# A one-layer streaming encoder with a mixture of experts: an expert's slots in another order, and the last products on another engine

## The chip, the cores and the metric

The kernel runs on one core of one Trainium2 chip. Such a core has a matrix engine (TensorE, PE in the profile), three engines for elementwise work (VectorE = DVE, ScalarE = ACT, GpSimd = POOL), an engine that here only issues transfers (SyncE = SP), and 16 DMA engines that move data between HBM and the on-chip memory (SBUF). The metric is the device time of one execution in microseconds (us). Before the change it is 1167.24 us, the median of three runs (1166.24 to 1170.16).

## The reference

There are 1104 tokens of width 1024: 64 of a sample stream, 16 learned ones, and 1024 of a prompt. They pass through one layer. A token mixer comes first (an input projection, pooling windows, gated linear attention, an output projection), then a mixture of experts:

```python
p_group = softmax(x @ w_rg + b_rg)                    # 4 groups, the best one is taken
le_sel  = the 8 expert logits of that group           # (T, 8)
top_v, top_i = lax.top_k(softmax(le_sel), 2)          # two experts per token
gates   = p_g * top_v / sum(top_v)
h       = silu(xb @ w_eg[e]) * (xb @ w_eu[e])         # per expert e of 32: 1024 -> 512, twice
ys      = h @ w_ed[e]                                 # 512 -> 1024
out[token] = sum over its two experts of gate * ys
```

A last RMSNorm follows: `y * rsqrt(mean(y*y) + 1e-6) * norm_final`. All values are f32. Outputs are the normalized rows of prompt and sample and the new states of pooling and attention.

## The kernel before

The 1104 tokens and 48 padding rows stand in nine tiles of 128 rows (`TILES`; the first holds the sample, the padding and the 16 learned tokens). The program has three stages.

**Mixer and router** (to about 530 us): a loop over the tiles. For each tile DVE also works out, for both picks of each token, its expert and its rank, which is the number of earlier picks of that expert (`back_rank`, L915 to L930). A tile's normalized rows are stored to `hn_rows` in HBM, once for each pick. To turn ranks into lists, L929 compares each rank with the constant row `iota_block`, which has 96 entries (`BLOCK`), one for each slot of an expert. That gives a 0/1 matrix `at_rank` of tokens by slots, and the matrix engine multiplies it with a table of row numbers (`mark`, L1292 to L1296). Summed over the tiles this is `idx_i`, 96 slots by 32 experts: the row number of the pick in that slot, or `NO_ROW` (4096) where the slot is empty. The constant row holds 0, 1, ..., 95, so that rank r stands in slot r, and the empty slots are the last ones.

**Experts** (about 530 to 1115 us): one expert after the other, 0 to 31, with two sets of buffers, b = e mod 2.
- SP loads the three weight matrices, 2 MB each, into the arena (`load_weights`, L383 to L393): `w_eg` of expert e once the matrix engine is through with `w_eg` of expert e-2, and likewise `w_eu` and `w_ed`. So every weight transfer is issued when its buffer comes free, and the three of one expert stand in one queue behind each other.
- POOL issues two indirect transfers for each expert: `gather` (L470 to L475) reads the rows named by column e of `idx_i` from `hn_rows` into a buffer of 96 partitions, one slot to a partition; `scatter` (L477 to L486) writes the results of the 96 slots back to `pick_rows` in HBM. Both have `bounds_check` with `oob_is_err=False`: a slot with `NO_ROW` moves no row.
- The matrix engine transposes the rows (L1149), multiplies by `w_eg` and `w_eu` (`up`, L1369) and by `w_ed` (`down`, L1380 and L1386). ACT and DVE form silu and the products in between, ACT takes the result out of PSUM.

There is code for experts with more than 96 picks (`slots`, `table`, the blocks under `n_x > 0`). With the given inputs the router gives every expert 50 to 88 picks, 2208 in all, so these blocks are jumped over.

**Last stage** (from about 1115 us): SP loads the two result rows of each token (L429), 18 transfers. For every tile DVE adds them, weighted with the gates, to the residual (`combine`, two instructions, L1125 and L1127). ACT squares and sums the row and forms 1/rms (L722 to L724). For tiles 0, 2, 4, 6 and 8 DVE multiplies by 1/rms and by `norm_final` in one instruction (`normalize`, L1133). For tiles 1, 3, 5 and 7 ACT multiplies by 1/rms (L727) and POOL by `norm_final` (L523). SP stores the tiles in order (L433, L435), each when its semaphore `out_ready` is up.

Of the kernel before, what the change touches and what calls it, by code (L numbers as in the profile page):

```python
# [24 lines left out]
ALU = mybir.AluOpType  # L25
ACT = mybir.ActivationFunctionType
# [10 lines left out]
TILES = (SAMPLE + PADS + META + SEQ) // P  # L37
# [21 lines left out]
BLOCK = 96  # L59
# [5 lines left out]
PICK_ROWS = PICKS * TILES * P  # L65
OUT_ROWS = [SAMPLE] + [P] * (TILES - 1)
NO_ROW = 4096
BIG = 3.0e38

# [19 lines left out]
def constants():  # L90
    c = np.zeros((P, N_CONST), np.float32)
    p = np.arange(P)[:, None]
    t = np.arange(P)[None, :]

    def put(name, v):
        c[:, COL[name][0]:COL[name][1]] = v

    put("ident", p == t)
    put("keep", np.arange(PAIRS * P)[None, :] % CHUNK != 0)
    put("causal", (p <= t) & (p // CHUNK == t // CHUNK))  # L100
    put("before", p < t)
    put("count_fix", np.concatenate([w / np.minimum(np.arange(META) + 1, w) for w in WINDOWS])[None, :])
    put("iota_block", np.arange(BLOCK)[None, :])
    put("iota_e", np.arange(NE)[None, :])
    put("first_g", GROUPS - np.arange(GROUPS)[None, :])
    put("first_e", PER_GROUP - np.arange(PER_GROUP)[None, :])
    put("pick", p + TILES * P * np.arange(PICKS)[None, :] - NO_ROW)
    put("valid", (p < SAMPLE) | (p >= SAMPLE + PADS))
    put("block_edge", BLOCK * (1 + np.arange(EXTRA_PER_E))[None, :])
    put("iota_x", np.arange(EXTRA)[None, :])  # L110
    put("edge_x", BLOCK * np.arange(EXTRA)[None, :])
    return c
# [40 lines left out]
def build(nc, x_all, state_pool, state_gla, norm_mix, w_in, w_gate_up, b_gate, w_pool, pool_scale, gla_norm, w_out,  # L153
# [5 lines left out]
    with ExitStack() as ctx:  # L159
        def sb(name, shape, dt=F32):  # L160
            return ctx.enter_context(nc.sbuf_tensor(name, shape, dt))

        def sem(name):
            return ctx.enter_context(nc.semaphore(name))
# [15 lines left out]
        def con(name, rows=P):  # L180
            return cst[0:rows, COL[name][0]:COL[name][1]]
# [114 lines left out]
        def lot(n):  # L296
            return arena[:, n * D:(n + 1) * D]
        y1 = [lot(2 * i) for i in range(TILES)]
        y2 = [lot(2 * i + 1) for i in range(TILES)]
        g_fin = lot(2 * TILES)  # L300
        fss = sb("fss", [P, TILES])
# [10 lines left out]
            parted dve_front dve_back dve_once dve_moe dve_fin act_front act_back act_once act_fin history_kept pool_steps  # L312
            pe_eT pe_g pe_u2 pe_d sig_ready hid_ready eT_ready ye_ready row_idx_ready
            x_tab_dve x_tab_pe x_idx_ready x_w x_rows x_pe x_dve x_act x_stored x_pool pick_idx_ready
            fin_ready frstd_ready scaled_ready g_fin_in""").split()
        s = {n: sem(n) for n in names}
        g_in = [sem(f"g_in{b}") for b in range(2)]
        u_in = [sem(f"u_in{b}") for b in range(2)]
# [4 lines left out]
        out_ready = [sem(f"out_ready{i}") for i in range(TILES)]  # L323
# [116 lines left out]
        def _(pool):  # L440
# [77 lines left out]
                                                     bounds_check=PICK_ROWS - 1, oob_is_err=False).then_inc(s["x_stored"], 16)  # L518
                        wait_parted(pool, s["x_stored"], 16 * n + 16, s["parted"])

            for i in range(1, TILES, 2):
                pool.wait_ge(s["scaled_ready"], (i + 1) // 2)
                nc.gpsimd.tensor_tensor(y2[i], y2[i], g_fin, ALU.mult).then_inc(out_ready[i], 1)  # L523

        @block.scalar
        def _(act):
            A = nc.scalar.activation
# [3 lines left out]
            final = Steps(act, s["act_fin"])  # L532
# [186 lines left out]
            for i in range(TILES):  # L719
                act.wait_ge(s["fin_ready"], i + 1)  # L720
                r = OUT_ROWS[i]
                final.then(A(y2[i][0:r, :], y1[i][0:r, :], ACT.Square, scale=D ** -0.5, accum_out=fss[0:r, i:i + 1]))  # L722
                final.then(A(fss[0:r, i:i + 1], fss[0:r, i:i + 1], ACT.Ln, bias=eps[0:r, 0:1]))
                rstd_i = A(fss[0:r, i:i + 1], fss[0:r, i:i + 1], ACT.Exp, scale=-0.5)  # L724
                if i % 2:
                    final.then(rstd_i)
                    A(y2[i], y1[i], ACT.Copy, scale=fss[:, i:i + 1]).then_inc(s["scaled_ready"], 1)  # L727
                else:
                    rstd_i.then_inc(s["frstd_ready"], 1)

        @block.vector
        def _(dve):
# [13 lines left out]
            V.tensor_copy(token[:, :], con("pick")).then_inc(s["setup_dve"], 1)  # L747
            V.memset(idx_f[:, :], float(NO_ROW)).then_inc(s["idx_added"], 1)
            def x_turned(i, first=False):

                if not first:
                    dve.wait_ge(s["pe_v"], i)
                for half in range(2):
                    dve.wait_ge(s["pe_xT"], 2 * i + half + 1)
                    k = slice(half * KD // 2, (half + 1) * KD // 2)
                    V.tensor_tensor(xnT[:, k, :], bank[half][:, :].rearrange("p (k n) -> p k n", n=P),
                                    g_mix[:, k].unsqueeze(2).to_broadcast([P, KD // 2, P]), ALU.mult).then_inc(s["xnT_ready"], 1)
# [115 lines left out]
            def first_of(step, values, top, order, marks, out, valid=None):  # L873

                step.then(V.tensor_reduce(top, values, AX.X, ALU.max))
                step.then(V.scalar_tensor_tensor(out=marks, in0=values, scalar=top, in1=order, op0=ALU.is_ge, op1=ALU.mult))
                step.then(V.tensor_reduce(rt[:, 0:1], marks, AX.X, ALU.max))
                if valid is None:
                    step.then(V.tensor_scalar(out, marks, rt[:, 0:1], None, ALU.is_equal))
                else:  # L880
                    step.then(V.tensor_scalar(out, marks, rt[:, 0:1], valid, ALU.is_equal, ALU.mult))

            def back_route(j, first=False):
# [9 lines left out]
                first_of(back, le[:, 0, :], rt[:, 2:3], con("first_e"), le[:, 2, :], oh[:, 0, :])  # L893
                back.then(V.scalar_tensor_tensor(out=le[:, 1, :], in0=oh[:, 0, :], scalar=-BIG, in1=le[:, 0, :], op0=ALU.mult, op1=ALU.add))
                first_of(back, le[:, 1, :], rt[:, 3:4], con("first_e"), le[:, 3, :], oh[:, 1, :])
# [170 lines left out]
            once.then(V.tensor_copy(token[:, :], con("pick")))  # L1066
            once.then(V.memset(idx_xf[:, :], float(NO_ROW)))

# [51 lines left out]
            final = Steps(dve, s["dve_fin"])  # L1120
# [7 lines left out]
                                       op0=ALU.mult, op1=ALU.add).then_inc(s["fin_ready"], 1)  # L1128

            def normalize(i):  # L1130
                dve.wait_ge(s["frstd_ready"], i // 2 + 1)
                r = OUT_ROWS[i]
                V.scalar_tensor_tensor(out=y2[i][0:r, :], in0=y1[i][0:r, :], scalar=fss[0:r, i:i + 1], in1=g_fin[0:r, :],  # L1133
                                       op0=ALU.mult, op1=ALU.mult).then_inc(out_ready[i], 1)

            dve.wait_ge(s["g_fin_in"], 16)
            for i in range(TILES):
                combine(i)
                if i % 2:
                    normalize(i - 1)  # L1140
            normalize(TILES - 1)

# [349 lines left out]
```

## Time and profile before

| what | value |
|---|---|
| median of three runs | 1167.24 us |
| the profiled execution: its time, its span | 1166.75 us, 1164.9 us |
| PE busy | 1042.9 us, 90% of the span |
| DVE, ACT, POOL busy | 426.3, 247.0, 118.8 us |
| moved by DMA | 262.08 MB, mean 225 GB/s |
| weights of one expert | 3 x 2048 KB |

The span runs from the first to the last instruction, and the execution's own time is 1.85 us longer. The profile gives busy time by engine, 40 equal slices of the span (29.1 us each) with the share in which the 16 DMA engines were busy, and the chain of work that ended last, followed back from the end. "DMA share" in a table of stretches is the mean busy share of the 16 DMA engines; packets that overlap on one engine can bring it a little over 1.

### The profile page before, as it was taken

The numbers are of one execution on the slowest core, as the hardware profiler recorded it, in microseconds if no ns is written. First come the engines' busy times: TensorE is split into PE (matmuls) and PEld (weight loads), VectorE is DVE, ScalarE is ACT, GpSimd is POOL, SyncE is SP. The second block draws the span as 40 slices with busy tenths as digits, with TensorE's granted clock in tenths as the row PEclk, the third lists the DMA queues.
The fourth block names the chain that finished last, engine by engine and source line by source line (L and its number), as shares of the span: only waits on it lengthen the run. The fifth ranks groups of instructions, "written<-read, shape, count | busy, mean of one in ns | idle before, by whom it ended". The sixth has DMA issues, their size and how long they took to land.

```text
span 1164.9 us, 31332 instructions
## 1 busy us (share of the span) xinstructions
PE 1042.9 (90%) x13842; PEld 853.9 (73%) x13842; DVE 426.3 (37%) x914; ACT 247.0 (21%) x510; POOL 118.8 (10%) x178
## 2 busy tenths in 40 slices
PE   5999999999999999866999999998988888899910
PEld 5778786868687777636888988897877777787810
DVE  1426162625345362622523322332313132322347
ACT  2333232222323131210111111111111101010124
POOL 0110101010010101001111111111110101010012
PEclk9999999999999999977999999999999999999965
DMA  8900000000000000574999999999999999999566
GB/s 280 360 1 37 0 36 36 0 36 0 36 0 36 0 36 1 205 306 157 376 379 390 391 400 380 387 390 368 370 370 356 374 353 372 353 372 353 214 240 246
DMA packets 50844, 262.08 MB, mean 225 GB/s; under 512 B 8205, under 2 KB 10701, under 8 KB 42618
## 3 DMA queue, kind: packets, MB, share of 16 engines
q1 hardware_dynamic: 41050, 234.05, 53.2%
q0 software_dynamic: 7168, 18.10, 4.6%
q10 hardware_dynamic: 2592, 9.44, 2.0%
q8 instruction: 26, 0.43, 0.1%
q14 instruction: 8, 0.07, 0.0%
HBM read 241.84 MB, written 26.80 MB: 231 GB/s over the span
## 4 chain that ended last, share of the span: by engine, by line
PE 62%; DMA 24%; DVE 10%; issue 2%; ACT 1%; SPq 0%; ACTq 0%; DVEq 0%; POOLq 0%; POOL 0%
DMA arena<-in_w_eg 22%; PE bank L1369 19%; PE bank L1161 17%; PE bank L1270 11%; PE bank L1380 5%; PE bank L1386 2%; PE bank L1149 2%; DVE er L815 2%; PE bank L1239 2%; DVE arena L1125 1%; DVE arena L1127 1%; DMA arena<-in_w_in 1%; PE bank L1263 1%; DVE hnT L870 1%; PE bank L1257 1%
## 5 line engine op out<-in xcount | busy, mean ns | idle before, releaser
L1161 PEld LDWEIGHTS bank<-xnT,arena 128*128 128x128 f32 x1728 | 198.0, 193 | 11.8 <-issue 7.6
L1161 PE MATMUL bank<-xnT,arena 128*128 128x128 f32 x1728 | 199.3, 277 | 3.7 <-DMA arena<-in_w_in 3.7
L1369 PEld LDWEIGHTS bank<-xnT,arena 128*64 128x64 f32 x4096 | 171.1, 138 | 16.0 <-DMA arena<-in_w_eg 9.9
L1369 PE MATMUL bank<-xnT,arena 128*64 128x96 f32 x4096 | 174.2, 248 | 8.8 <-DMA arena<-in_w_eg 7.1
L1369 PEld LDWEIGHTS bank<-hnT,arena 128*64 128x64 f32 x4096 | 169.9, 137 | 14.2 <-issue 14.2
L1369 PE MATMUL bank<-hnT,arena 128*64 128x96 f32 x4096 | 172.8, 246 | 7.0 <-DMA arena<-in_w_eg 6.9
L1009 DVE TENSOR_SCALAR mixT<-mixT 128x384 f32<-128x384 f32 x32 | 11.5, 361 | 355.0 <-ACT mixT L685 355.0
L1270 PE MATMUL bank<-arena,mixT 128*128 128x512 f32 x288 | 126.9, 599 | 2.9 <-DVE mixT L856 2.9
L1270 PEld LDWEIGHTS bank<-arena,mixT 128*128 128x128 f32 x288 | 54.7, 192 | 69.3 <-issue 65.6
L1380 PE MATMUL bank<-arena,osq 128*32 128x384 f32 x768 | 88.2, 495 | 9.0 <-DMA arena<-in_w_ed 9.0
L1380 PE MATMUL bank<-arena,silu_r 128*32 128x384 f32 x768 | 85.8, 488 | 7.6 <-DMA arena<-in_w_ed 7.1
L1386 PE MATMUL bank<-arena,osq 128*32 128x256 f32 x384 | 87.7, 385 | 0.0
L1386 PE MATMUL bank<-arena,silu_r 128*32 128x256 f32 x384 | 85.9, 380 | 0.0
L1010 DVE RECIPROCAL mixT<-mixT 128x384 f32<-128x384 f32 x32 | 81.7, 2553 | 1.1
L1211 PE MATMUL bank<-arena,xnT 128*128 128x512 f32 x144 | 65.3, 597 | 0.0
L861 DVE TENSOR_TENSOR h_all<-bank,h_all 128x512 f32 (+1 forms) x9 | 6.2, 692 | 145.6 <-PE bank L1270 145.6
L690 ACT ACTIVATE kz_v<-bank 96x384 f32<-96x384 f32 x32 | 13.8, 482 | 187.2 <-PE bank L1386 187.2
L453 POOL TENSOR_TENSOR window_work<-window_work 128x568 f32<-128x568 f32 x9 | 10.2, 1132 | 422.5 <-ACT window_work L583 422.5
L1386 PEld LDWEIGHTS bank<-arena,osq 128*32 128x32 f32 x384 | 41.4, 111 | 15.5 <-issue 0.8
L690 ACT ACTIVATE hs<-bank 96x384 f32<-96x384 f32 x32 | 13.8, 482 | 181.3 <-PE bank L1386 181.3
L1386 PEld LDWEIGHTS bank<-arena,silu_r 128*32 128x32 f32 x384 | 41.0, 110 | 15.0
L1380 PEld LDWEIGHTS bank<-arena,osq 128*32 128x32 f32 x768 | 31.7, 111 | 20.3 <-issue 11.3
(197 smaller groups left out, 1030.0 us busy)
## 6 DMA issues: line engine op xcount, KB each, us to landing
arena<-in_w_eg SPq DMA_DIRECT2D x32, 2048.0 KB, 28.3
arena<-in_w_eu SPq DMA_DIRECT2D x32, 2048.0 KB, 28.1
arena<-in_w_ed SPq DMA_DIRECT2D x32, 2048.0 KB, 27.9
hn_rows<-hs ACTq DMA_DIRECT2D x18, 512.0 KB, 3.4
arena<-pick_rows SPq DMA_DIRECT2D x16, 512.0 KB, 10.3
arena<-in_w_in SPq DMA_DIRECT2D x3, 2048.0 KB, 14.6
arena<-in_w_out SPq DMA_DIRECT2D x1, 4096.0 KB, 25.0
out_y_prompt<-arena SPq DMA_DIRECT2D x8, 512.0 KB, 2.8
```

Of the source, the lines that this page charges most:

```text
L690: A(ye[b][:, half * OWN:(half + 1) * OWN], bank[6 + half][0:BLOCK, 0:OWN], ACT.Copy).then_inc(s["ye_ready"], 1)
L815: front.then(V.reciprocal(flat, flat))
L870: V.tensor_tensor(hnT[:, k, :], bank[half][:, :].rearrange("p (k n) -> p k n", n=P), g_ffn[:, k].unsqueeze(2).to_broadcast([P, KD // 2, P] ...
L1010: moe.then(V.reciprocal(gs[:, 0:NH], gs[:, 0:NH]))
L1149: return nc.tensor.transpose(out, src, ident[0:n, 0:n])
L1161: last = mm(out, w_in_sb[:, k, a:b], xnT[:, k, :], start=k == 0, stop=k == KD - 1)
L1211: last = mm(bank[6][:, :], xnT[:, k, :], w_in_sb[:, k, V0:R0], start=k == 0, stop=k == KD - 1)
L1239: last = mm(out[:, 2 * p * DV:(2 * p + 2) * DV], kz[:, c, p, :], v_sb[:, 2 * p * DV:(2 * p + 2) * DV], start=True, stop=True)
L1270: last = mm(bank[half][:, :], mixT[:, k, :], w_out_sb[:, k, half * 512:(half + 1) * 512], start=k == 0, stop=k == KD - 1)
L1369: last = mm(out[q * SW:(q + 1) * SW, n * BLOCK:(n + 1) * BLOCK], w[:, k, m * P + q * SW:m * P + (q + 1) * SW], rowsT[b][:, k, :], start=k ...
L1380: last = mm(bank[6 + half][g * TG:(g + 1) * TG, 0:OWN], tokens(k, g), wd[b][:, k, half * OWN:(half + 1) * OWN], start=k == 0, stop=k == KF ...
L1386: return mm(bank[n][TGS * TG:P, c:c + REST], tokens(k, g), wd[b][:, k, 2 * OWN:D], start=k == 0 and c == 0, stop=k == KF - 1, skip_group_c ...
```

## The change

Two things are changed. The constant row `iota_block` now holds 16 * (s mod 6) + s div 6 for slot s. Rank r therefore stands in slot 6 * (r mod 16) + r div 16: rank 0 in slot 0, rank 1 in slot 6, rank 15 in slot 90, rank 16 in slot 1. Before, 69 picks filled slots 0 to 68; now they fill the first five of the six slots 6n to 6n+5 for n = 0 to 4, and the first four for n = 5 to 15. The instructions that make and use the lists stay the same. In the last stage POOL's four products and ACT's four scalings go, and DVE normalizes all nine tiles.

```diff
+SPREAD = 16
+RUN = BLOCK // SPREAD
...
-    put("iota_block", np.arange(BLOCK)[None, :])
+    put("iota_block", (SPREAD * (np.arange(BLOCK) % RUN) + np.arange(BLOCK) // RUN)[None, :])
...
-            for i in range(1, TILES, 2):
-                pool.wait_ge(s["scaled_ready"], (i + 1) // 2)
-                nc.gpsimd.tensor_tensor(y2[i], y2[i], g_fin, ALU.mult).then_inc(out_ready[i], 1)
...
-                rstd_i = A(fss[0:r, i:i + 1], fss[0:r, i:i + 1], ACT.Exp, scale=-0.5)
-                if i % 2:
-                    final.then(rstd_i)
-                    A(y2[i], y1[i], ACT.Copy, scale=fss[:, i:i + 1]).then_inc(s["scaled_ready"], 1)
-                else:
-                    rstd_i.then_inc(s["frstd_ready"], 1)
+                A(fss[0:r, i:i + 1], fss[0:r, i:i + 1], ACT.Exp, scale=-0.5).then_inc(s["frstd_ready"], 1)
...
             def normalize(i):
-                dve.wait_ge(s["frstd_ready"], i // 2 + 1)
+                dve.wait_ge(s["frstd_ready"], i + 1)
...
             for i in range(TILES):
                 combine(i)
-                if i % 2:
+                if i:
                     normalize(i - 1)
             normalize(TILES - 1)
```

On DVE in the last stage, the end of the program before, from the second instruction of tile 6 on (L1125 and L1127 combine, L1133 normalizes; `arena` holds the rows, `gate_all` the gates, `fss` 1/rms):

```order
L1127 SCALAR_TENSOR_TENSOR arena<-arena,gate_all 128x1024
L1125 SCALAR_TENSOR_TENSOR arena<-arena,gate_all,h_all 128x1024
L1127 SCALAR_TENSOR_TENSOR arena<-arena,gate_all 128x1024
L1133 SCALAR_TENSOR_TENSOR arena<-arena,fss 128x1024
L1125 SCALAR_TENSOR_TENSOR arena<-arena,gate_all,h_all 128x1024
L1127 SCALAR_TENSOR_TENSOR arena<-arena,gate_all 128x1024
L1133 SCALAR_TENSOR_TENSOR arena<-arena,fss 128x1024
```

The same place now, where the lines are L1119, L1121 and L1127:

```order
L1121 SCALAR_TENSOR_TENSOR arena<-arena,gate_all 128x1024
L1127 SCALAR_TENSOR_TENSOR arena<-arena,fss 128x1024
L1119 SCALAR_TENSOR_TENSOR arena<-arena,gate_all,h_all 128x1024
L1121 SCALAR_TENSOR_TENSOR arena<-arena,gate_all 128x1024
L1127 SCALAR_TENSOR_TENSOR arena<-arena,fss 128x1024
L1119 SCALAR_TENSOR_TENSOR arena<-arena,gate_all,h_all 128x1024
L1121 SCALAR_TENSOR_TENSOR arena<-arena,gate_all 128x1024
L1127 SCALAR_TENSOR_TENSOR arena<-arena,fss 128x1024 x2
```

A normalizing instruction now stands behind every pair from tile 1 on, and at the end stand those of tiles 7 and 8; there are four more of them in all. On ACT the end of the program before, tiles 7 and 8 (L722 squares and sums, L723 and L724 form 1/rms, L727 scales the row):

```order
L722 ACTIVATE arena,fss<-arena 128x1024
L723 ACTIVATE fss<-fss,eps 128x1
L724 ACTIVATE fss<-fss 128x1
L727 ACTIVATE arena<-arena,fss 128x1024
L722 ACTIVATE arena,fss<-arena 128x1024
L723 ACTIVATE fss<-fss,eps 128x1
L724 ACTIVATE fss<-fss 128x1
```

The same two tiles now:

```order
L721 ACTIVATE arena,fss<-arena 128x1024
L722 ACTIVATE fss<-fss,eps 128x1
L723 ACTIVATE fss<-fss 128x1
L721 ACTIVATE arena,fss<-arena 128x1024
L722 ACTIVATE fss<-fss,eps 128x1
L723 ACTIVATE fss<-fss 128x1
```

The scaling between the tiles is gone, and POOL's last instructions, `L523 TENSOR_TENSOR arena<-arena 128x1024 x4`, with it. The order on PE and SP is the same as before.

## Rows read from the trace of the kernel before

**Rows 1.** The page: its slices' DMA lines, and the chain that ended last.
```profile
DMA  8900000000000000574999999999999999999566
GB/s 280 360 1 37 0 36 36 0 36 0 36 0 36 0 36 1 205 306 157 376 379 390 391 400 380 387 390 368 370 370 356 374 353 372 353 372 353 214 240 246
...
PE 62%; DMA 24%; DVE 10%; issue 2%; ACT 1%; SPq 0%; ACTq 0%; DVEq 0%; POOLq 0%; POOL 0%
```

**Rows 2.** The chain in order of time: start us, us, what.
```profile
606.34 10.71 PE bank L1369 x256
623.18 10.71 PE bank L1369 x256
640.02 10.71 PE bank L1369 x256
...
673.69 10.71 PE bank L1369 x256
...
774.73 5.46 PE bank L1369 x128
780.34 31.24 DMA arena<-in_w_eg
811.63 5.53 PE bank L1369 x128
817.32 31.93 DMA arena<-in_w_eg
...
1094.81 10.71 PE bank L1369 x256
```

**Rows 3.** Stretches: us, busy us of each engine (instructions), PE clock, DMA share, GB/s.
```profile
570.00:780.00 210.00, 209.47 (x4180) 182.71 (x4174) 66.61 (x96) 31.83 (x77) 31.34 (x51) 1.00 1.01 387
780.00:1060.00 280.00, 250.50 (x4915) 217.17 (x4912) 78.14 (x105) 35.30 (x85) 33.82 (x58) 0.99 0.99 366
```

**Rows 4.** Issues of w_eg at 595, 763 and 840-860 us: KB, us to landing.
```profile
arena<-in_w_eg SPq DMA_DIRECT2D x1, 2048.0 KB, 12.8
...
arena<-in_w_eg SPq DMA_DIRECT2D x1, 2048.0 KB, 29.2
...
arena<-in_w_eg SPq DMA_DIRECT2D x1, 2048.0 KB, 32.2
```

**Rows 5.** SP in order of time: one issue of w_eg.
```profile
645.63 0.33 SPq L385 DMA_DIRECT2D arena<-in_w_eg  x1
```

**Rows 6.** The page's DMA queues: packets, MB, time as share of 16 engines' span.
```profile
q1 hardware_dynamic: 41050, 234.05, 53.2%
q0 software_dynamic: 7168, 18.10, 4.6%
```

**Rows 7.** Stretches of 2 us with and without row transfers, columns as in rows 3.
```profile
630.00:632.00 2.00, 2.00 (x56) 2.00 (x52) 2.00 (x1) 0.00 (x0) 0.00 (x0) 1.00 1.02 412
...
634.00:636.00 2.00, 2.00 (x30) 1.50 (x33) 1.32 (x3) 0.00 (x0) 0.00 (x0) 1.00 1.01 299
...
640.00:642.00 2.00, 2.00 (x51) 2.00 (x52) 0.00 (x0) 1.86 (x5) 0.00 (x0) 1.00 1.00 412
...
915.00:917.00 2.00, 2.00 (x54) 2.00 (x52) 1.52 (x3) 0.00 (x0) 0.00 (x0) 1.00 1.00 334
...
921.00:923.00 2.00, 2.00 (x32) 1.42 (x28) 0.00 (x0) 0.00 (x0) 0.00 (x0) 1.00 0.97 305
```

**Rows 8.** POOL's gather issued at 628.31 us: us to landing.
```profile
xs<-hn_rows,rows_idx POOLq DMA_INDIRECT x1, 9.5
```

**Rows 9.** Last stage in order of time: start us, us, engine, line, operation, idle before.
```profile
1123.39 1.28 DVE L1125 SCALAR_TENSOR_TENSOR arena<-arena,gate_all,h_all 64x1024 f32<-64x1024 f32 x1 [15.86 <-DMA arena<-pick_rows]
...
1129.60 1.27 DVE L1125 SCALAR_TENSOR_TENSOR arena<-arena,gate_all,h_all 128x1024 f32<-128x1024 f32 x1
...
1131.50 2.90 POOL L523 TENSOR_TENSOR arena<-arena 128x1024 f32<-128x1024 f32 x1 [16.20 <-ACT arena L727]
1132.11 3.38 DVE L1125 SCALAR_TENSOR_TENSOR arena<-arena,gate_all,h_all 128x1024 f32<-128x1024 f32 x1
...
1155.88 1.28 DVE L1127 SCALAR_TENSOR_TENSOR arena<-arena,gate_all 128x1024 f32<-128x1024 f32 x1
1156.45 2.91 POOL L523 TENSOR_TENSOR arena<-arena 128x1024 f32<-128x1024 f32 x1 [5.41 <-ACT arena L727]
...
1158.94 1.51 DVE L1133 SCALAR_TENSOR_TENSOR arena<-arena,fss 128x1024 f32<-128x1024 f32 x1 [1.78 <-ACT fss L724]
```

**Rows 10.** Last stage by line: xcount, busy us, mean ns, idle before.
```profile
L1125 DVE SCALAR_TENSOR_TENSOR arena<-arena,gate_all,h_all 128x1024 f32<-128x1024 f32 (+1 forms) x9 | 17.8, 1975 | 15.9 <-DMA arena<-pick_rows 15.9
```

**Rows 11.** SP's loads of the result rows, and the stretch that they fill.
```profile
1117.83 11.23 SPq L429 DMA_DIRECT2D arena<-pick_rows  x18
...
1120.00:1140.00 20.00, 0.00 (x0) 0.00 (x0) 16.44 (x12) 8.88 (x18) 3.09 (x2) 0.50 1.01 386
```

More of the change, by code:

```diff
@@ L314, in build @@
             x_tab_dve x_tab_pe x_idx_ready x_w x_rows x_pe x_dve x_act x_stored x_pool pick_idx_ready
-            fin_ready frstd_ready scaled_ready g_fin_in""").split()
+            fin_ready frstd_ready g_fin_in""").split()
         s = {n: sem(n) for n in names}
```

## The prediction

> **What bounds the kernel now.** I read the page first: the slices, then the chain of waits. The DMA engines are 90% busy or more from slice 20 to slice 37, and the chain puts 62% of the span on PE and 24% on DMA [rows 1]. A mean over stages with different limits says little, so the chain in order of time came next [rows 2]. It changes its nature in the middle of the expert stage. Up to 774.73 us every expert starts 16.84 us after the one before (606.34 to 774.73 us is ten experts): PE is bound by its own work. After that, every second expert ends on a 31 to 33 us wait for `w_eg`, and the starts of experts 14 and 31, at 774.73 and 1094.81 us, lie 17 experts and 320.1 us apart, 18.83 us each. At PE's own pace they would lie 286.3 us apart. So 33.8 us is the most that faster transfers can give in this stage.
>
> Why does DMA fall behind only then? The time from issue to landing of `w_eg` answers it [rows 4]. An issue waits for its buffer, so in PE's rhythm it comes a fixed time before its use: that of 645.63 us is for the expert that starts at 673.69 us, 28.1 us later [rows 5, 2]. It lands after 12.8 us for expert 5 and after 29.2 us for expert 15. So each expert's weights land 1.64 us later than the last, and DMA's pace is 16.84 + 1.64 = 18.48 us per expert from the start; the lead is merely used up at expert 15. In the stretches the DMA share stays at 1.01 and 0.99, while the rate falls from 387 to 366 GB/s [rows 3]. Work, or disturbance, on the engines that finish last is therefore what can be won.
>
> The last stage is a third regime: from 1123.39 us DVE runs without a gap, apart from one wait of 1.78 us before its last instruction [rows 9].
>
> **The order of the slots.** Nothing is added in this stage: the constant has other values, and the same instructions read it. What can move is which DMA engine carries which row. The POOL queue shows 7168 packets and 18.10 MB [rows 6]. 7168 is 64 transfers of 112; 18.10 MB is 4416 rows of 4 KB, and the router's counts, worked out from the given inputs, sum to 2208 picks, moved twice. So an empty slot moves no row, but has a packet, and 112 is 96 slots and one more packet for each of 16 engines. 
>
> The Trainium skill ("DMA: Bandwidth & Descriptors", "Why a DMA increments its semaphore by 16 and not by 1") gives consecutive shares: a DMA of 96 partitions uses 16 engines, the first share on the lowest-numbered; no run here shows it. Another section of the page, "The descriptor swizzle", has a formula for 128 partitions that would give the first eight engines eight slots each and the others four; by it the busiest engine would go from 16 rows to about 11.5, and the result would be that of the first rival.
>
> A row's price: 4.6% of 16 engines' 1164.9 us is 857 us for 4416 rows, 0.194 us each [rows 6]. 2.5 rows fewer are 0.485 us per expert. All of it lies on the engines that end last, if the mapping holds.
>
> The rows also disturb. In stretches of 2 us in which none is on its way the rate is 412 GB/s; towards the end of a gather that was issued at 628.31 us and landed 9.5 us later it is 299, and in the late half stretches at 305 and 334 GB/s lie further apart [rows 7, 8]. How much is that? The busiest engine moves 6.29 MB / 16 + 12 x 4 KB = 442 KB per expert; at a sixteenth of 412 GB/s that is 17.18 us, and 18.48 is what it takes: 1.30 us of disturbance. With at most 4.75 rows instead of 6 in a transfer I let it shrink in that ratio, by 0.27 us. The bounds are nothing, and all of 1.30, since engines in step might not disturb each other; growth is the last rival. I take the value near the lower end, because the number of rows stays the same.
>
> New pace: 18.48 - 0.485 - 0.27 = 17.72 us, 0.88 more than PE's. From expert 5 to 31 the landing time grows 26 x 0.88 = 22.9 us to 35.7 us, 7.6 more than the 28.1 that PE can bear. Expert 31 starts 33.8 - 7.6 = **26.2 us earlier**. With nothing off the disturbance it is 19.0 us, with most of it gone all 33.8. The wait that replaces the present one is the same, for `w_eg`, from about expert 22 on.
>
> **The last stage.** Three of POOL's four products each stall a DVE instruction: the one at 1132.11 us takes 3.38 instead of 1.28 us and ends 1.1 us behind POOL's product, which had started 0.6 us earlier [rows 9]. By line, L1125 has 17.8 us where nine of 1.28 are 11.5: 6.3 us of stalls [rows 10]. The fourth product costs the last normalization 0.23 us (1.51 against 1.28). On the other side stand four more normalizations of DVE. Five of its instructions, from 1123.39 to 1129.60 us, take 6.21 us, 1.242 each. Before the last tile's pair ends there are now 18 + 7 of them: 31.05 us, to 1154.44 us, where it is 1157.16 now. The last normalization still waits 1.78 us behind the pair for ACT, with that of tile 7 hidden in the wait; it starts at 1156.22 and ends at 1157.50 instead of 1160.45 us: **2.9 us earlier**. The other new waits, for 1/rms of the odd tiles, cost nothing: it is there 1.78 us after a pair, and another pair (2.48 us) stands in between; only the next pair is queued behind. POOL's and ACT's removed work is off the path otherwise. The loads are no new bound: 18, 8.9 MB, at 386 GB/s end near 1141 us, and the last tile's pair starts at 1152 [rows 11]. If tile 7's normalization were not covered, 1.2 us would be lost. The bounds are 0.5 us (stores now one by one on DVE's rhythm) and 4 us.
>
> **Sum.** Against the profiled execution's own 1166.75 us (span 1164.9 and 1.85 around it): 1166.75 - 26.2 - 2.9 = 1137.6 us. The median of the runs is 0.5 us higher, so **1138 us**.
>
> **Rivals.**
> 1. PE's pace throughout. With the engines in step most of the disturbance goes, and the pace is under 16.84 us. For it: 412 GB/s would bring an expert's 6.86 MB in 16.65 us. Against it: the disturbed stretches are there at 634 us already [rows 7], before the lead is used up. 1166.75 - 33.8 - 2.9 + 0.5 = 1130.5 us. Chance 0.22.
> 2. Nothing is won in the expert stage: DMA is bound by bytes, or the slots are already dealt out evenly. For it: a DMA share of 0.99 leaves little that could be filled, and the bytes are the same. Against it: 387 GB/s over 210 us at the same share shows that 366 is no ceiling [rows 3]. Only the last stage gains: 1164.3 us. Chance 0.10. The Trainium skill ("HBM Reference", "Specifications (TRN2)") puts the effective rate per core at about 358 GB/s, by which this rival would hold; the 387 measured goes beyond that, and the page itself says that a core streaming alone does.
> 3. Slower: the rows now come on all 16 engines, so that no engine's weights run undisturbed. If the stretch near 325 GB/s grows from some 8 us of an expert's time (915 to 923 us) to 16, each expert loses 8 x (1 - 325/412) = 1.7 us against 0.49 gained; the pace from the start becomes 19.7 us, and expert 31 is 26 x 2.86 + 12.8 - 28.1 = 59 us late instead of 33.8: about 1189 us. It decides from a stretch 2.3 us longer than now. Against it: fewer rows per engine make a transfer shorter. Chance 0.05.
> 4. Part of it: the row time alone or less, 1145 to 1160 us. Chance 0.18.
>
> My forecast's own case, 1132 to 1145 us, has 0.45. The range that leaves out 2 in 10 is 1129 to 1157 us. About 0.3% (3.5 us) is what a measurement of this kernel tells from no change; rival 2 lies inside it, so: faster 0.85, within 0.10, slower 0.05.
>
> **What would show it.** In the changed profile the landing time of `w_eg` for expert 15 should be 20 to 23 us instead of 29.2, the stretch from 570 to 780 us stay near 390 GB/s, and that from 780 to 1060 us come close to it; the first long wait for `w_eg` should stand behind expert 20. If the landing time grows as before, the mapping or the mechanism is wrong. If it does not grow, rival 1 holds. If the rate is lower in both stretches, rival 3 does. In the last stage all 18 L1119 and L1121 should take 1.28 us, and DVE's last instruction 1.28.

## The result, and the profile after

The changed kernel takes 1128.56 us (median of four runs, 1128.18 to 1130.37), the kernel before 1166.74 us (median of four runs, 1164.63 to 1170.16). The ratio is 0.967, with an interval from 0.965 to 0.970. The forecast was 1138 us with a range from 1129 to 1157 us: the direction was right, the gain, 38 us, was a third larger than the 28.7 that were forecast, and the time lies just below the low end. PE's pace throughout, the outcome of the first rival, is what happened, though not in the way that the rival gave for it (below).

The profiled execution after took 1130.37 us, with a span of 1128.4 us. The page's slices and chain come first, as those of [rows 1].

```profile
DMA  8900000000000000076799999999999999999557
GB/s 277 384 2 38 0 37 0 37 0 37 16 21 37 0 37 1 38 299 218 254 397 367 406 404 402 413 408 396 409 402 398 411 405 396 412 397 395 238 198 304
...
PE 84%; DVE 10%; DMA 2%; issue 2%; ACT 1%; SPq 0%; ACTq 0%; DVEq 0%; POOLq 0%; POOL 0%
```

The DMA engines look as busy as before, and yet DMA has gone from 24% of the chain to 2%. The rate no longer falls in the second half of the expert stage; it stays near 400 GB/s. The chain in order of time (start us, us, what) shows the same at the first multiplication of an expert:

```profile
608.37 10.71 PE bank L1363 x256
625.21 10.71 PE bank L1363 x256
...
776.76 10.71 PE bank L1363 x256
793.60 10.71 PE bank L1363 x256
...
1063.02 10.71 PE bank L1363 x256
```

Experts 4 and 31 start at 608.37 and 1063.02 us. That is 27 experts in 454.65 us, 16.84 us each: PE's own pace up to the last expert. The waits for `w_eg` of 31 to 33 us in [rows 2] are gone. PE's list of waits between 530 and 1080 us (line, releaser: us in total, times, longest us) names no weights at all; its one DMA wait is for the first expert's rows:

```profile
PE bank L1143 <- DMA window_work<-hn_rows,rows_idx: 5.9, 1, 5.9
PE bank L1363 <- issue: 2.0, 3, 1.2
PE bank L1374 <- issue: 1.0, 2, 0.5
```

In the kernel before, the same list, between 540 and 1112 us, began with the weights:

```profile
PE bank L1380 <- DMA arena<-in_w_ed: 16.1, 14, 2.0
PE bank L1369 <- DMA arena<-in_w_eg: 14.0, 15, 1.2
```

The two stretches of [rows 3] now read (columns as there):

```profile
570.00:780.00 210.00, 209.28 (x4156) 181.83 (x4147) 68.25 (x99) 31.87 (x77) 29.19 (x49) 1.00 1.01 398
780.00:1060.00 280.00, 280.00 (x5601) 245.25 (x5601) 88.49 (x119) 40.31 (x97) 39.57 (x66) 1.00 1.01 401
```

The DMA share is 1.01 in both, where it was 1.01 and 0.99, while the rate rose from 387 to 398 and from 366 to 401 GB/s.

In the last stage every one of DVE's combining and normalizing instructions now takes 1.28 us, and the last normalization waits 0.58 us where it waited 1.78 [rows 9, 10]. By line (xcount, busy us, mean ns, idle before):

```profile
L1121 DVE SCALAR_TENSOR_TENSOR arena<-arena,gate_all 128x1024 f32<-128x1024 f32 (+1 forms) x9 | 11.6, 1284 | 0.3
L1127 DVE SCALAR_TENSOR_TENSOR arena<-arena,fss 128x1024 f32<-128x1024 f32 (+1 forms) x9 | 11.5, 1279 | 0.6 <-ACT fss L723 0.6
L1119 DVE SCALAR_TENSOR_TENSOR arena<-arena,gate_all,h_all 128x1024 f32<-128x1024 f32 (+1 forms) x9 | 11.5, 1277 | 15.5 <-DMA arena<-pick_rows 15.5
```

The first combining instruction and the last two normalizations, in order of time:

```profile
1091.22 1.28 DVE L1119 SCALAR_TENSOR_TENSOR arena<-arena,gate_all,h_all 64x1024 f32<-64x1024 f32 x1 [15.46 <-DMA arena<-pick_rows]
...
1122.22 1.28 DVE L1127 SCALAR_TENSOR_TENSOR arena<-arena,fss 128x1024 f32<-128x1024 f32 x1
...
1124.09 1.28 DVE L1127 SCALAR_TENSOR_TENSOR arena<-arena,fss 128x1024 f32<-128x1024 f32 x1 [0.58 <-ACT fss L723]
```

So the 36.5 us between the two spans (1164.9 and 1128.4) come out as follows. The first combining instruction starts 32.2 us earlier (1123.39 and 1091.22). From there to the end of the last normalization it is 37.06 us before and 34.15 after: 2.9 us. From there to the end of the span it is 4.45 us before and 3.03 after: 1.4 us more.

### The profile page after: what moved, and what is told of

It is laid out like the page before. It is cut to its first block, busy times and chain, and to the rows that moved or that the text cites. A ratio compares the mean times of both kernels' runs of the same rounds, so it can differ in the third digit from the quotient of the medians.

```text
span 1128.4 us, 31328 instructions
## 1 busy us (share of the span) xinstructions
PE 1041.3 (92%) x13842; PEld 853.4 (76%) x13842; DVE 424.4 (38%) x918; ACT 242.5 (21%) x506; POOL 107.2 (10%) x174
## 4 chain that ended last, share of the span: by engine, by line
PE 84%; DVE 10%; DMA 2%; issue 2%; ACT 1%; SPq 0%; ACTq 0%; DVEq 0%; POOLq 0%; POOL 0%
PE bank L1363 31%; PE bank L1155 17%; PE bank L1264 11%; PE bank L1374 10%; PE bank L1380 5%; PE bank L1143 4%; DVE er L809 2%; PE bank L1233 2%; DVE arena L1121 1%; DVE arena L1119 1%; DVE arena L1127 1%; DMA arena<-in_w_in 1%; PE bank L1257 1%; DVE hnT L864 1%; PE bank L1251 1%
## 5 line engine op out<-in xcount | busy, mean ns | idle before, releaser
L1380 PEld LDWEIGHTS bank<-arena,osq 128*32 128x32 f32 x384 | 40.8, 110 | 15.0
L1205 PEld LDWEIGHTS bank<-arena,xnT 128*128 128x128 f32 x144 | 26.1, 190 | 26.3 <-issue 26.3
```

The lines of the kernel that those rows point to most:

```text
L1205: last = mm(bank[6][:, :], xnT[:, k, :], w_in_sb[:, k, V0:R0], start=k == 0, stop=k == KD - 1)
L1380: return mm(bank[n][TGS * TG:P, c:c + REST], tokens(k, g), wd[b][:, k, 2 * OWN:D], start=k == 0 and c == 0, stop=k == KF - 1, skip_group_c ...
```

## The experiments

Unless said otherwise, an edit stands against the changed kernel. Ratios are against the kernel before, run beside it on the same chip; its medians there were 1162 to 1165 us.

### One part of the change at a time

`slots_only` is the kernel before with the new `iota_block`; `tail_only` is the changed kernel with the old one:

```diff
-    put("iota_block", (SPREAD * (np.arange(BLOCK) % RUN) + np.arange(BLOCK) // RUN)[None, :])
+    put("iota_block", np.arange(BLOCK)[None, :])
```

> The kernel before with the new order of the slots alone; the last stage stays as it was. Theory A (the DMA engine with the most rows sets when weights land; the new order brings it from 12 rows per expert to 9.5, and DMA then keeps PE's pace): about 33 us less than before, 1133 to 1136 us, with no wait of PE for w_eg, and the landing time of w_eg no longer growing. Theory B (the two parts need each other): less than 30 us.

> The changed kernel with the old order of the slots (rank r in slot r), so the last stage's part alone. From the two traces: DVE's work from first combine to last normalization 37.06 -> 34.15 us, and from its end to the end of the span 4.45 -> 3.03 us. So 3 to 4.5 us less than before, 1162 to 1164 us. If the shorter end after DVE's last instruction belongs to the expert stage and not to the last stage, 3 us or less.

`slots_only` took 1132.07 us, ratio 0.973 (0.971 to 0.975), and PE waited for no weights. `tail_only` took 1159.36 us, ratio 0.995 (0.994 to 0.997). So the order of the slots brings 31 to 33 us (1159.36 to 1128.56; 1164.74 to 1132.07), and the last stage 3.5 to 5.4 us (1132.07 to 1128.56; 1164.74 to 1159.36): the expert stage's gain is the slots' alone.

`slots_only` also has the landing times that the trace after lacks for `w_eg`. Its DMA issues in windows about 578, 746 and 982 us (experts 5, 15 and 29; KB, us to landing) read, one row each:

```profile
arena<-in_w_eg SPq DMA_DIRECT2D x1, 2048.0 KB, 13.4
...
arena<-in_w_eg SPq DMA_DIRECT2D x1, 2048.0 KB, 14.8
...
arena<-in_w_eg SPq DMA_DIRECT2D x1, 2048.0 KB, 18.0
```

Where [rows 4] grow from 12.8 to 29.2 us in ten experts, this grows by 4.6 us in 24, 0.19 us per expert. DMA's pace is then 16.84 + 0.19 = 17.03 us per expert, where 17.72 had been forecast. It is still slower than PE, but of the 28.1 us of lead the stage leaves about ten unused. (The lead is the time from the issue of `w_eg` to its use in PE's rhythm.)

### How many engines carry six rows

These three keep every instruction and every row, and deal the slots out in other ways (the names behind `#` are not part of the code). `reverse` mirrors the old order, so that the last engines are full and the first one empty. `spread8` lets used and skipped slots alternate too, but in twelves: with 69 picks eight or nine slots are used, then four or three skipped, so that, in blocks of six, eight of the 16 engines have six rows. `one_heavy` gives the first six ranks to the first six slots and deals the rest out evenly: one engine has six rows, the others four or five.

```diff
+    put("iota_block", (BLOCK - 1 - np.arange(BLOCK))[None, :])                                # reverse
+    put("iota_block", (8 * (np.arange(BLOCK) % 12) + np.arange(BLOCK) // 12)[None, :])        # spread8
+    slot = np.arange(BLOCK)                                                                  # one_heavy
+    put("iota_block", np.where(slot < RUN, slot, RUN + (SPREAD - 1) * (slot % RUN) + slot // RUN - 1)[None, :])
```

> The changed kernel with rank r in slot 95 - r: the used slots stand together at the end instead of the beginning, so the rows are as uneven over blocks of six slots as in the kernel before (six rows in the busiest block, none in the emptiest), but they lie in other partitions. Theory A (the busiest of 16 engines, each serving six neighbouring slots): as the last stage's part alone, 1160 to 1166 us. Theory C (which SBUF partitions the gathered rows are written to sets the disturbance: slots 0 to 68 are half of the partitions again and again): a large part of the gain, 1130 to 1150 us.

> The changed kernel with consecutive ranks twelve slots apart instead of six (rank r in slot 12 * (r mod 8) + r div 8): used and empty slots alternate and lie over all 96 partitions, but of each pair of blocks of six the first is always full and the second has about 2.6 rows. Theory A (the busiest engine's row count): 12 rows per expert as before, so hardly better than the last stage's part alone, 1155 to 1166 us. Theory D (it is the mixing of used and empty slots, or their spread over all partitions, that helps): as the changed kernel, 1127 to 1133 us. If engines serve twelve slots or slots one by one, it would be near the changed kernel too.

> The changed kernel, but the first six slots are always full (ranks 0 to 5) and the other ranks are dealt over the other fifteen blocks of six: engine 0 has 12 rows per expert as in the old order, every other engine about 8.4. Theory A (the row count of the busiest engine alone): as the last stage's part alone, about 1159 us. Theory E (the price is the disturbance while many engines are out of step and many rows meet, and one engine more or less does little): near the changed kernel, 1128 to 1140 us. Both in part: between, with the landing of the weights late by what one engine's 2.5 rows cost, 0.5 us per expert.

`reverse` took 1146.93 us (0.984, from 0.981 to 0.987), `spread8` 1151.12 us (0.990, from 0.988 to 0.992), `one_heavy` 1129.21 us (0.970, from 0.967 to 0.973). `reverse` lies in the range of the theory that partitions matter, which a run below tests; `spread8` lies 4 us below the range of the theory of the busiest engine. Alternation of used and skipped slots is not what counts in the main: `spread8` alternates and gets back 8 of the 31 us. Its issues of `w_ed` at 587.22 and 755.61 us, ten experts apart, land after

```profile
arena<-in_w_ed SPq DMA_DIRECT2D x1, 2048.0 KB, 15.3
...
arena<-in_w_ed SPq DMA_DIRECT2D x1, 2048.0 KB, 25.4
```

that is 1.01 us later per expert, a pace of 17.85 us. In the kernel before, the two of 589.68 and 758.08 us were

```profile
arena<-in_w_ed SPq DMA_DIRECT2D x1, 2048.0 KB, 12.8
...
arena<-in_w_ed SPq DMA_DIRECT2D x1, 2048.0 KB, 27.9
```

or 18.35, and after, those of 591.73 and 995.86 us, 24 experts apart,

```profile
arena<-in_w_ed SPq DMA_DIRECT2D x1, 2048.0 KB, 12.4
...
arena<-in_w_ed SPq DMA_DIRECT2D x1, 2048.0 KB, 16.8
```

or 17.02.

For `one_heavy`, whose time alone would say that a full engine costs nothing, the view has the landing of every second `w_ed` only. Its issues of 608.02, 776.42 and 1012.17 us (experts 5, 15 and 29) land after

```profile
arena<-in_w_ed SPq DMA_DIRECT2D x1, 2048.0 KB, 13.7
...
arena<-in_w_ed SPq DMA_DIRECT2D x1, 2048.0 KB, 17.1
...
arena<-in_w_ed SPq DMA_DIRECT2D x1, 2048.0 KB, 31.1
```

that is 0.34 us later per expert at first, 1.00 in the fourteen experts after, and 0.73 over all 24, a pace of 17.57. After the change, the same three experts' issues (608.56, 776.95 and 1012.70 us) land after

```profile
arena<-in_w_ed SPq DMA_DIRECT2D x1, 2048.0 KB, 13.8
...
arena<-in_w_ed SPq DMA_DIRECT2D x1, 2048.0 KB, 13.7
...
arena<-in_w_ed SPq DMA_DIRECT2D x1, 2048.0 KB, 17.5
```

or -0.01 us per expert at first and 0.15 over all 24. And the PE of `one_heavy`, by the list of waits up to 1090 us, does begin to wait for weights, but only in experts 28 and 29, 2.8 us in all:

```profile
PE bank L1375 <- DMA arena<-in_w_ed: 1.9, 2, 1.0
...
PE bank L1364 <- DMA arena<-in_w_eg: 0.9, 2, 0.5
```

So a single engine with six rows costs 0.35 us per expert over the first ten of these experts and 0.73 - 0.15 = 0.58 over all 24; the price forecast for 2.5 rows on the busiest engine (0.485) lies between the two. The lead of the transfers covers nearly all of it: 24 times 0.58 us is 14 us, about ten were left over, and the waits are the rest. My theory in its plain form, that the time follows the busiest engine, failed on this run; the pace follows it, the time only where the lead is gone. With a mean of 69 picks, none, one, eight and eleven engines with six rows (the changed kernel, `one_heavy`, `spread8`, the kernel before) go with 16.83, 17.18, 17.85 and 18.35 us over ten experts (4 to 14 or 5 to 15).

`reverse` remains odd. Its counts per engine are those of `tail_only`, eleven with six rows, its rates 390 and 379 GB/s against 387 and 369, and it is 12 us faster; its time lies near that of `spread8` with eight. So the number of full engines is not all. Which of them are full matters somewhat; these runs do not say why.

### The price of the rows with DMA as the bound

To read DMA's own pace, PE must not set the rhythm. In the kernels named `half_` the gate and up products of an expert take half of their steps:

```diff
-                    for k in range(KD):
+                    for k in range(KD // 2):
```

Each is a single execution. The pace is the time between SP's issues of `w_eg` for experts 15 and 31, divided by 16. In `half_old` and `half_new`, for example (start us, us, queue):

```profile
751.72 3.90 SPq L388 DMA_DIRECT2D arena<-in_w_eg  x1
...
1048.34 4.05 SPq L388 DMA_DIRECT2D arena<-in_w_eg  x1
```

```profile
746.91 0.95 SPq L388 DMA_DIRECT2D arena<-in_w_eg  x1
...
1027.77 0.65 SPq L388 DMA_DIRECT2D arena<-in_w_eg  x1
```

which are 18.54 and 17.55 us per expert. `half_none` has no rows at all (`iota_block` is -1), `half_old_gather` and `half_old_scatter` have the old order and rows in one of the two transfers alone, with a list of empty slots for the other.

> The old order of the slots, and TensorE leaves out half of the products with w_eg and w_eu (four of eight parts of the inner dimension), so that PE needs some 11.5 us per expert and DMA is bound all through the expert stage; all transfers stay. It shows DMA's own pace. Starts of experts 5 and 31 should be 18.5 to 18.9 us per expert apart, as in the late half of the kernel before.

> The same with the new order: DMA's own pace, which the changed kernel hides behind PE's 16.84 us. The prediction's sum says 17.7 us per expert, which the changed kernel already contradicts. Theory A with the rows' price alone: 18.0. Theory E (most of the disturbance goes with engines in step): 16.2 to 16.8 us, and rates over 400 GB/s.

> The same with all slots empty: the constant row holds -1, so no rank matches, gathers and scatters are issued but move no row, and the last stage loads the rows of the normalized input instead. It shows the weights' own pace, the floor under both orders. At 412 GB/s (stretches without rows of the kernel before) 6.29 MB take 15.3 us per expert. If the old order's pace over this floor is near 12 rows of 0.19 us (2.3 us), the rows cost what their packets take and do not disturb; if it is 3.3 us or more, a third of their price is disturbance.

> As half_old (half of the products with w_eg and w_eu left out, DMA bound all through; 18.54 us per expert between the issues of w_eg for experts 15 and 31, with no rows 15.01), but the scatters move no row (their list of slots is all empty) and the last stage loads the rows of the normalized input. If the gather makes the whole disturbance: 15.0 + 6 rows of 0.16 to 0.19 us + 1.3 to 1.5 = about 17.4 us. If gather and scatter share alike: 16.8 us.

> As half_old, but the gathers move no row (their list is all empty, the matrix engine works on what lies in the buffers). If the gather makes the whole disturbance: 15.0 + 6 rows = 16.0 to 16.2 us per expert. If they share alike: 16.8 us. If it is the scatter: 17.4 us.

| kernel | us per expert | whole kernel, us |
|---|---|---|
| `half_none` | 15.01 | 1053.0 |
| `half_old_scatter` | 15.79 | 1075.3 |
| `half_new_gather` | 16.76 | 1101.7 |
| `half_full_gather` | 17.45 | 1124.7 |
| `half_old_gather` | 17.46 | 1117.7 |
| `half_new` | 17.55 | 1123.7 |
| `half_heavy` | 17.81 | 1132.5 |
| `half_reverse` | 18.08 | 1137.6 |
| `half_old_shift32` | 18.09 | 1150.7 |
| `half_old` | 18.54 | 1151.5 |

Of the expectations, `half_new` misses Theory E's range and comes nearest to the prediction's own 17.7, and `half_old_gather` fits a gather that makes the whole disturbance. The weights alone take 15.01 us. Old scatters add 0.78 us, old gathers 2.45 us. The rate in stretches of 2.5 us from 800 to 900 us, first of `half_old_scatter`, then of `half_old_gather`, shows what kind of cost it is:

```profile
GB/s 423 406 400 419 444 424 433 419 388 415 442 441 421 416 377 395 436 441 418 429 415 398 413 462 411 426 431 344 408 456 428 433 416 387 411 444 438 418 429 406
```

```profile
GB/s 315 369 428 431 369 405 444 418 403 298 339 356 398 406 298 329 393 426 393 413 447 346 311 315 390 406 402 411 290 339 395 408 336 388 447 439 343 298 346 362
```

With scatters the rate runs more evenly: one stretch of the 40 lies under 370 GB/s, with gathers eighteen do. From 740 to 960 us (columns as in [rows 3]) `half_none` and then `half_old_scatter` have the same 419 GB/s, so that scatters add little but their bytes:

```profile
740.00:960.00 220.00, 174.07 (x3048) 139.38 (x3048) 72.26 (x100) 37.13 (x90) 32.80 (x57) 1.00 1.01 419
```

```profile
740.00:960.00 220.00, 174.13 (x2898) 137.65 (x2894) 71.85 (x98) 34.81 (x84) 32.63 (x56) 0.95 1.01 419
```
With gathers the rate breaks down to about 300 GB/s about once per expert. The disturbance of [rows 7] is in the main the gather's; gather and scatter alone add 3.23 us together, and both at once 3.53.

The new order brings the price of the gather from 2.45 to 1.75 us (`half_new_gather`), 0.71 of it, near the 4.75 / 6 = 0.79 of the rows on the busiest engine. Is it that engine's count, or the number of rows, or that some engines have none? `half_full_gather` is `half_old_gather` with an entry in all 96 slots, so that nearly every engine moves six rows; two entries point past the end, and 94 rows are moved for each expert (12.33 MB on the POOL queue in 32 transfers):

```diff
-    put("pick", p + TILES * P * np.arange(PICKS)[None, :] - NO_ROW)
+    put("pick", p + TILES * P * np.arange(PICKS)[None, :])
...
-            V.memset(idx_f[:, :], float(NO_ROW)).then_inc(s["idx_added"], 1)
+            V.tensor_copy(idx_f[:, :], con("pick", BLOCK)[:, 0:1].to_broadcast([BLOCK, NE])).then_inc(s["idx_added"], 1)
```

> As half_old_gather (17.46 us per expert; 2.45 over the 15.01 without rows), with the new order. If a gather's price goes by the rows of the busiest engine (4.75 instead of 6): 15.01 + 2.45 x 0.79 = 16.95. If it goes by the number of rows in all (the same 69): 17.46. If engines with equal work stay in step and disturb each other for a shorter time: less than 16.8.

> As half_old_gather, but the empty slots are filled: their entries name a row of their own, and all entries are moved on by their slot's number (so other rows are gathered; a few past the end are left out). Every engine then gathers six rows for each expert, 96 in all instead of 69, and none is idle. By the rows of the busiest engine: 17.46 as half_old_gather. By the number of rows in all: 15.01 + 2.45 x 96 / 69 = 18.4. If being in step is worth more than the added rows cost: under 17.3.

`half_full_gather` has 17.45 us, with 94 rows, as `half_old_gather` has 17.46 with 69; both issue `w_eg` of expert 31 within 2 us of each other (1024.76 and 1022.90 us). The whole kernels differ by 7 us, 5 of them behind that issue and not explained. In these two runs the count of the fullest engines sets the gather's price; rows added on the others cost next to nothing.

The prediction took its mapping, six neighbouring slots to an engine, without a view. The Trainium skill ("DMA: Bandwidth & Descriptors", "Why a DMA increments its semaphore by 16 and not by 1") gives a DMA of 96 partitions 16 engines, the first share on the lowest-numbered, and does not say how the slots of an indirect transfer are shared out. The paces above agree with six neighbouring slots, but they do not refute the other mapping that the prediction names: by it the gathers of `half_full_gather` and `half_old_gather` also have equally many rows, eight, on their fullest engines, and one, three and eight engines have eight in `one_heavy`, `spread8` and the old order. The trace decides between them. In the first gather of `half_full_gather`, from 530.36 to 532.22 us, no other queue moves anything, and its record holds 94 packets of 4 KB and 18 of 4 bytes. Linked where one packet starts within 5 ns of another's end, they form runs, one engine's packets in a row. At least five of these, more by how near ties are linked, are exactly six rows with one 4-byte packet behind, and none has the eight rows that the other mapping asks for.

Another rival was that not engines but the places in memory that the rows land in matter. `half_old_shift32` moves the gathered rows from partitions 0 to 95 to partitions 32 to 127:

```diff
-                nc.gpsimd.indirect_dma_start(rows[b], None, hn_dram, ...
+                nc.gpsimd.indirect_dma_start(rows[b][P - BLOCK:P, :], None, hn_dram, ...
```

> As half_old, but the gathered rows are written to partitions 32 to 127 instead of 0 to 95 (the matrix engine turns them with a product that picks these partitions): every DMA engine has the same rows as in half_old, only the place in SBUF differs; with about 69 of 96 slots used it is partitions 32 to 100 instead of 0 to 68. Theory C (which partitions are written sets the disturbance): 17.3 to 18.0 us per expert instead of 18.54. Theory A or F: 18.4 to 18.7 us.

It issued the weights of expert 31 at 1048.57 us, `half_old` at 1048.34, and the whole kernels differ by 0.8 us. By this run the partitions make no difference. The two paces, 18.09 and 18.54, differ through the first of the two marks (759.09 and 751.72 us): issues come in uneven pairs, so a pace from one execution is sure to some 0.4 us. By the issues of `w_ed` for the same experts the two are 18.36 and 18.52.

> As half_new (17.55 us per expert), with the order of one_heavy: engine 0 has 12 rows per expert, the others about 8.4. If the busiest engine's packets are what counts there: 17.55 + 2.5 x 0.19 = 18.0. If nothing: 17.55. If one straggler is enough to bring all of the old order's price back: 18.5.

> As half_old (18.54 us per expert), with the order of reverse (slot 95 - r): as many rows on the busiest engines, other partitions and other engines. If row counts are all: 18.5. The run reverse was 12 us faster than tail_only, so if that belongs to DMA's own pace: about 18.0.

`half_heavy` (`one_heavy`'s order) lies 0.26 us above `half_new`, less than expected and within that uncertainty; by the issues of `w_ed` it is 0.67 (17.99 and 17.32). `half_reverse` lies 0.46 us below `half_old`, 0.60 by `w_ed` (17.92 and 18.52); its whole time, 14 us shorter, supports `reverse`, without a cause.

### Shorter packets of weights

If a row of 4 KB loses because it takes turns with larger packets, smaller ones should help the old order. `old_4k` is `tail_only` with `w_eg` and `w_eu` each in four transfers of 512 KB, whose runs are 4 KB long:

```diff
-                sp.dma_start(wg[b], w_eg[bass.ds(e * D, D), :].rearrange("(p k) n -> p k n", k=KD)).then_inc(g_in[b], 16)
+                for j in range(0, KD, 2):
+                    sp.dma_start(wg[b][:, j:j + 2, :], w_eg[bass.ds(e * D, D), :].rearrange("(p k) n -> p k n", k=KD)[:, j:j + 2, :]).then_inc(g_in[b], 16)
```

> Old order of the slots with the last stage's part (as tail_only, 1159.4 us), but w_eg and w_eu are loaded by four transfers of 512 KB each, in runs of 4 KB instead of 16 KB per partition, so that a row on the POOL queue takes turns with 4 KB packets of weights all the time, and not with 16 KB ones. Theory F (the disturbance lasts as long as the rows of a transfer take to get through, and that is longest where each waits for a 16 KB packet; the old order loses its lead, comes into that phase and then loses more): most of the gain of the new order without it, 1130 to 1145 us. Theory A or C (row counts, partitions): 1155 to 1170 us; smaller packets alone make the weights a little slower, since a packet's time does not fall quite in proportion.

It took 1148.22 us (0.987, from 0.985 to 0.990), 11 us less than `tail_only` (9 by the two ratios), and missed both theories' ranges. So about a third of the loss goes with the size of the weights' packets or with the finer split, which this run does not separate. It stays behind the changed kernel, and no version here that does all of the work beat that one.

## Why the prediction was wrong in size

- **What bounds the kernel.** Right. The cause was DMA's pace from the beginning of the stage on, not a second regime: with the pace at 17.0 instead of 18.5 us the regime of waits never comes.
- **The rows on the busiest engine, 0.485 us per expert.** Right in size, as far as the runs show, with the mapping that it stood on: `one_heavy` puts six rows back on one engine and loses 0.35 us per expert over ten experts and 0.58 over 24.
- **"I take the value near the lower end, because the number of rows stays the same."** This is the step that failed. The disturbance was let shrink by 0.27 us of its 1.30. By `w_eg`'s landing the pace fell from 18.48 to 17.03, 1.45 us; without the 0.485 it leaves 0.96 us, three quarters of the disturbance. The number of rows was the wrong reason: `half_full_gather` shows that the rows on the less filled engines cost next to nothing. The bound "all of 1.30" was stated; the choice between the bounds had no row behind it. Why three quarters of the disturbance went stays open.
- **"So each expert's weights land 1.64 us later than the last."** This is a mean of an uneven growth, and it made the forecast's start too slow. Between the rows of experts 5 and 15 [rows 4] stands that of expert 13, the issue of 729.84 us before:

```profile
arena<-in_w_eg SPq DMA_DIRECT2D x1, 2048.0 KB, 23.3
```

  The landing time grows by 1.31 us per expert up to there and by 2.95 in the last two. From the even part the same sum gives 16.84 + 1.31 - 0.485 - 0.27 = 17.40 us, which is just inside the edge of 17.43 worked out below, with no wait for `w_eg`. So this reading and the disturbance together put the forecast on the wrong side. `one_heavy` shows the same bend, 0.34 us per expert up to a landing time of 17.1 us and 1.00 behind it: where transfers are late already, the pace is slower. These runs do not say why.
- **The ratio 4.75 / 6.** Not refuted where DMA is the bound: there the gather's price shrank to 0.71, and the pace by 0.99 us (18.54 to 17.55), nearer to the 0.755 forecast than the 1.45 in PE's rhythm. What was added in PE's rhythm, about 0.46 us, was not isolated. Some of it belongs to the uneven growth: from the 18.15 of experts 5 to 13 before to the 16.98 of experts 5 to 15 in `slots_only` (13.4 to 14.8 us) it is 1.17 us.
- **The lead of 28.1 us.** Right as a quantity and as the deciding one: 12.8 + 0.19 x 26 is 17.7 us, far from 28.1, so no wait appears. The starts of experts 4 and 31 lay 488.47 us apart before [rows 2] and lie 454.65 after: 33.8 us, all that could be won. (The stage begins 2 us later after, 608.37 against 606.34 us for expert 4, which leaves 31.8 at expert 31.) The predicted "first long wait for `w_eg` behind expert 20" did not come; the landing time grew by 0.19 us per expert, next to nothing, and the sentence "If it does not grow, rival 1 holds" named the outcome.
- **Rival 1.** Its argument, that the pace falls under 16.84 us, did not hold: it is 17.0. Its time came out all the same, through the lead, a way that the prediction had not priced: any pace up to 16.84 + (28.1 - 12.8) / 26 = 17.43 us gives the same time. The forecast's 17.72 was 0.29 us beyond that edge. Its 0.22 was too small for a case whose edge lay so near.
- **The last stage, 2.9 us.** Right as far as it went: 37.06 to 34.15 us, all 18 L1119 and L1121 at 1.28 us. Not foreseen was 1.4 us behind it. Before, POOL's product of tile 7 and DVE's of tile 8 ended 1.1 us apart [rows 9], and both stores went out at the very end; after, DVE ends tile 7 at 1123.50 and tile 8 at 1125.37 us, and the first store is under way while the second is made.
- **Rivals 2 and 3.** Neither: the same bytes for each expert move at 401 instead of 366 GB/s, and even rows on all engines disturb less, not more.

Between the two spans, 36.5 us were won against 29.1 forecast. Of the missing 7.4 us, 6.0 lie ahead of the last stage (32.2 against 26.2), by the pace, and 1.4 behind its last normalization.

## What to carry to other kernels

Where transfers run ahead of their use, work out the pace at which the lead is used up just at the end, and see on which side of it a forecast lies: up to that edge a slower transfer is free, and beyond it every tenth of a microsecond counts once per step. Read the pace from several steps, not from two ends, since here it got worse as the lead ran out. A DMA share of 1.0 does not say that the bytes are the bound; compare rates between stretches, and ask which engine has the most pieces. As far as this kernel shows, the rows of an indirect transfer should be dealt out so that no engine has more than the others, and a gather deserves it before a scatter does.

## What the hardware showed that was not expected

- A gather of 69 rows of 4 KB costs 2.45 us of DMA time per expert, a scatter of the same rows 0.78 us, and with gathers the rate falls to about 300 GB/s in stretches of 2.5 us.
- A gather of 94 rows, six on nearly every engine, costs as much as one of 69 rows with six on eleven engines: 17.45 and 17.46 us per expert.
- The same kinds of transfers move at 366 or at 401 GB/s over 280 us with a DMA share of 0.99 and 1.01.
